# A decoder layer with a product-key expert stage: the two gate buffers of the V stage placed 128 bytes further on

## The reference, cut to what matters

```python
q = (xt @ w_pq)                                  # queries
s = einsum('thpd,hpkd->thpk', q, sub_keys)       # scores against 2 x 128 keys per head
... top-k, experts, gates = softmax(top_s)
u = take(expert_u, experts); act = gelu(einsum('tkd,td->tk', u, x))
v = take(expert_v, experts); y = einsum('tk,tkd->td', gates * act, v)
return rmsnorm(x + y, final_norm_gain)
```

## Time and profile before

| | |
|---|---|
| median of three runs | 2114.12 us (2106.12 to 2117.99) |
| the profiled execution | 2107.04 us |
| its span in the profile | 2105.3 us |
| PE busy | 2017.8 us, 96% |
| POOL, DVE, ACT busy | 1092.2, 1175.0, 903.8 us |
| granted clock of PE, mean | 0.982 of full speed |
| read from memory | 378.15 MB, 182 GB/s over the span |

### The profile page before, as it was taken

How to read it: one execution, slowest core, us unless ns; L and a number is a source line. 1 busy time by engine, 2 the same in 40 slices (tenths; PEclk the granted TensorE clock), 3 DMA queues, 4 the chain that set the end, 5 groups by cost and what they waited for, 6 DMA issues and landing times.

```text
span 2105.3 us, 36148 instructions
## 1 busy us (share of the span) xinstructions
PE 2017.8 (96%) x12814; PEld 1813.3 (86%) x12814; DVE 1175.0 (56%) x1942; ACT 903.8 (43%) x1132; POOL 1092.2 (52%) x450
## 2 busy tenths in 40 slices
PE   7798798997999999999999999999999999999996
PEld 6686687886899999999999999988888888888885
DVE  6568638125362993168888885035555555555555
ACT  6233234454543444544444444444444444444443
POOL 7576566785697888888888888850000000000001
PEclk9899899998999999999999999999999999999998
DMA  8343456554565666665555556676666665666563
GB/s 317 126 150 119 128 167 196 152 183 139 162 206 171 192 195 192 190 190 180 177 175 177 179 178 181 194 256 190 193 193 189 189 190 191 193 190 192 189 190 119
DMA packets 104753, 383.31 MB, mean 182 GB/s; under 512 B 12144, under 2 KB 12656, under 8 KB 103408
## 3 DMA queue, kind: packets, MB, share of 16 engines
q1 hardware_dynamic: 101232, 365.50, 55.1%
q10 hardware_dynamic: 3456, 16.89, 2.2%
HBM read 378.15 MB, written 4.19 MB: 182 GB/s over the span
## 4 chain that ended last, share of the span: by engine, by line
PE 69%; POOL 18%; issue 12%; DVE 1%; POOLq 0%; ACT 0%; DVEq 0%; ACTq 0%
PE ps L1215 22%; PE ps L1214 22%; PE ps L1213 22%; POOL wlo L363 18%; PE ps L1495 1%; PE ps L1469 0%; POOLq L362 0%; DVE x_back L1168 0%; DVE stats L634 0%; ACT big L608 0%; DVE stats L1179 0%; DVE big L1173 0%; POOLq L366 0%; ACT x_back L615 0%; PE ps L1521 0%
## 5 line engine op out<-in xcount | busy, mean ns | idle before, releaser
L363 POOL TENSOR_TENSOR wlo<-raw,whi 128x1024 fp32r<-128x1024 f32 x444 | 1086.3, 2450 | 314.7 <-ACT whi L413 311.1
L413 ACT ACTIVATE whi<-raw 128x1024 fp32r<-128x1024 f32 x436 | 462.4, 1062 | 768.4 <-PE ps L1215 765.6
L1213 PE MATMUL ps<-xh,whi 128*128 128x256 f32 x2176 | 601.6, 276 | 0.8 <-POOL wlo L363 0.8
L1214 PE MATMUL ps<-xl,whi 128*128 128x256 f32 x2176 | 600.8, 276 | 0.0
L1215 PE MATMUL ps<-xh,wlo 128*128 128x256 f32 x2176 | 600.8, 276 | 0.0
L1140 DVE TENSOR_TENSOR wlo<-raw,whi 128x1024 fp32r<-128x1024 f32 x248 | 304.3, 1227 | 336.6 <-ACT whi L566 336.6
L566 ACT ACTIVATE whi<-raw 128x1024 fp32r<-128x1024 f32 x256 | 271.1, 1059 | 390.5 <-PE ps L1215 390.5
L1213 PEld LDWEIGHTS ps<-xh,whi 128*128 128x128 f32 x2176 | 408.5, 188 | 1.2 <-issue 1.1
L1214 PEld LDWEIGHTS ps<-xl,whi 128*128 128x128 f32 x2176 | 408.5, 188 | 0.1
L1215 PEld LDWEIGHTS ps<-xh,wlo 128*128 128x128 f32 x2176 | 408.4, 188 | 0.0
L1215 PE MATMUL ps<-whi,gate_lo 128*128 128x512 f32 x1024 | 403.5, 394 | 0.0
(11 more groups left out here) (195 smaller groups left out, 1838.6 us busy)
## 6 DMA issues: line engine op xcount, KB each, us to landing
raw<-in_w_u SPq DMA_DIRECT2D x256, 512.0 KB, 3.5
raw<-in_w_v SPq DMA_DIRECT2D x256, 512.0 KB, 3.5
raw<-in_w_front SPq DMA_DIRECT2D x180, 512.0 KB, 3.5
big<-in_x_t ACTq DMA_DIRECT2D x4, 512.0 KB, 9.4
big<-in_x ACTq DMA_DIRECT2D x4, 512.0 KB, 5.6
big<-in_mem ACTq DMA_DIRECT2D x4, 512.0 KB, 5.5
big<-in_mem_t ACTq DMA_DIRECT2D x2, 1024.0 KB, 6.2
big<-in_x ACTq DMA_DIRECT2D x2, 1024.0 KB, 7.1
```

Source lines behind the costliest of these rows:

```text
L363: nc.gpsimd.tensor_tensor(wlo[:, j % SPL, :], raw[:, j % RAW, :], whi[:, j % SPL, :], ALU.subtract).then_inc(lo_done, 1)
L413: nc.scalar.activation(whi[:, j % SPL, :], raw[:, j % RAW, :], ACT.Copy).then_inc(hi_done, 1)
L1213: nc.tensor.matmul(out_ap, sh, mh, start=start, stop=False)
L1214: nc.tensor.matmul(out_ap, sh, ml, start=False, stop=False)
```

## The change

A buffer of 32 float32 (128 bytes), which nothing reads or writes, is put ahead of `gate_hi`, and the filler behind `gate_lo` is made 32 float32 shorter. So `gate_hi` and `gate_lo` move by 128 bytes, from offset 192 to offset 64, and all other buffers keep their places: `xh` and what follows start where they did, and the one-hot rows, which are laid out by an allocation of their own, too. No instruction is added, removed or moved, and no wait changes; every line number below the edit is one higher.

```diff
         of_u.close()
+        sb("gate_skew", [P, 32])
         gate_hi = sb("gate_hi", [P, 2, T], F32R)
         gate_lo = sb("gate_lo", [P, 2, T], F32R)
-        sb("rest_of_gates", [P, 576])
+        sb("rest_of_gates", [P, 544])
```

## The result

| | before | after |
|---|---|---|
| median of eight runs | 2114.7 us (2106.1 to 2118.0) | 2127.7 us (2118.0 to 2129.5) |
| ratio | | 1.0064, 95% interval 1.0044 to 1.0084 |
| profiled execution, span | 2107.04, 2105.3 us | 2118.00, 2116.2 us |
| first and last matmul of V | 1383.97, 2086.89 us | 1381.33, 2097.89 us |
| spacing in V | 228.9 ns | 233.3 ns |

The account below looks back on a forecast made before the run. PE's own pace was taken to bound the kernel, busy 96% of the span. V's spacing falling to 220.0 ns saves 27.3 us, other parts nothing: ratio 0.9870 times 2114.1 gives 2087 us, range 2078 to 2122.

Parts of the forecast that it names:

- That V is bound by PE's own pace: V stage: PE waits for nobody, so a change in its 228.9 ns matmul spacing passes to the end in full.
- the writes of the gate buffers: ACT and DVE writing the moved gates: even half as long again, covered by PE's work, cost nothing.
- That the period is 256 and the distance counts: PE's operand reads: the extra depends on stationary offset less moving offset, modulo 256; V goes from -64 to +64.
- They differ by 4.45 ns: Front and U, 256 columns: extras 11.1 at -64 and 6.7 ns at +64, laid to the sign of the distance.
- rows 6: Trace rows of the front's 256-column matmuls, `xh` stationary, distance -64: spacing 117.8 ns, extra 11.1.
- The four fit one simple form: All matmuls: fixed 6.7 ns, plus 4.45 per 256 columns at -64; V would fall to 220.0 ns, saving 27.3 us.
- rival B: V stage: half the gain, only the part beside the weight load goes, 4.45 ns a matmul, 13.7 us, 2100 us; chance 0.18.
- Rival C: V stage: slower, moving read meets weight load, at least 4.45 ns a matmul, 13.7 us, 2128 us; chance 0.17.
- rows 7: Trace rows of U's 256-column matmuls, weights stationary, `xh` moving, distance +64: spacing 113.3 ns, extra 6.7.
- Rival A: V stage: no change, period 128 or less, or the extra belongs to the moving operand alone; 2114 us, chance 0.29.
- rows 8: Trace rows of six 512-column matmuls at 1.2 GHz, 0.426 us apart without extra, taken to show an operand-fetch limit.
- a place in memory costs nothing: PE's operand reads: reading of the Trainium skill that speaks against any effect, making the sum 0.

Follow-up runs that it names:

- both half loads: V's stationary operands 64 columns instead of 128, against the changed kernel (gates at 64) and the one before (192): V spacing 232.7 and 228.3 ns.

## Why the prediction was wrong, step by step

**That V is bound by PE's own pace: right.** Every change of the spacing came through to the end in full. 13.6 us in V, 13.5 us by the ratio (0.64% of 2114). The tail, the writes of the gate buffers, U and the front cost nothing, as said.

**That the period is 256 and the distance counts: right.** The first was read from two stages that lie 256 apart, and the run 256 bytes on confirms it. The run with everything 64 bytes on shows the second.

**"They differ by 4.45 ns. What differs in kind is which of two operands is stationary, and with it the sign of the distance": this is the step that failed.** The difference between the earlier trace rows is not one between two arrangements. It is one between two paces, 113.3 and 117.8 ns, either of which a stretch of 256-column matmuls takes up and then keeps, with one placement. The tile of rows 6 has 113.3 in the profiles of the changed kernel and of the gates at 128, and U has 117.8 for its first stretch in six profiles (gates at 0 the second time, 128, 160, 256 bytes on, and both half loads) where `xh` was not moved relative to the weights. I had one execution, took two stretches that stood at different paces, and read the difference as a property of the code. The run with `xh` at 64 even agreed with the false rule in all its numbers. What the runs show in its place: at +64 V has 233.3 ns, an extra of 20.0 instead of the 6.7 that the rule gave, and U's 113.3 at the same distance says nothing on V.

**"The four fit one simple form": a chance fit.** Three extras and two constants. The form gave 220.0 ns, and nothing under 226.7 was seen with 512 columns. The argument against it was in my own rival B, that a form had to hold from 256 to 512 columns: it doesn't. Distance 0 is best at 512 and worst at 256, and 64 has the lowest value seen at 256 and is near the worst at 512.

**Rival C had the outcome, by luck.** Its mark was a spacing above 230 and its lower price 4.45 ns a matmul, 13.7 us, 2128 us; measured were 4.44 ns, 13.6 us, 2127.7. Its mechanism, though, is not shown. By it the moving read runs "into the place where the load began" because it starts close behind that place. Then distance 0, where the two begin together, should be bad as well, but it measured 226.7, the best, and 128 gained only 0.9 ns on 64. Its price was the 4.45 ns between rows 6 and rows 7, which belongs to two paces of 256-column matmuls. That V grew by the same 4.44 ns was not derived from anything, and no run shows why. What I held against it, that U has this distance and the smallest extra, is the failed step again. It had 0.17 by that argument, and the range ended at 2122, below its time.

**Rival A fell** with the first new placement. PE reads the gate buffers only in its weight loads. The writes of ACT and DVE into the gates move with them too, but they aren't the cause: between 252 and 272 us of the front nothing writes `xh` or `xl`, and the spacing there is 226.7 with `xh` at 0 and 233.3 at 64 and at 224, as in V. So the effect must come through the load beside the moving stream, and yet not in proportion to its length. What remains open is which circuit makes the steps, and why odd multiples of 32 stand at the top; the runs give the table and no law. Nor do rows 8 show that fetching operands is the limit: they show that the extra is gone at the lower clock, which a fixed cost hidden behind slower columns would do as well.

## What to carry to other kernels

The pace of a stream of matmuls at full clock can hang on the distance between the stationary and the moving operand modulo 256, here by 3.4% with 512 moved columns (226.7 to 234.3 ns) and by 5.9% with 256 (113.3 to 120.0), with no wait anywhere. If PE is the bound, try a few offsets per form of matmul and read the spacing of the starts. Do not carry a good distance from one form to another, and do not derive it from two stretches of one profile. First see in a second execution whether the stretch repeats. If it doesn't, the times of whole runs come in clumps, and the stage's own spacing tells what a single time can't.

## What the runs showed of the hardware that was not expected

- Most paces are a round number of cycles. At 2.4 GHz 226.7 ns are 544 cycles, 233.3 are 560, 228.9 are 549.3, which is 1648 for three. 113.3 are 272 and 120.0 are 288. Above the number of columns that is 32, 48, 37.3, 16 and 32 cycles. A steady pace can be a cycle over several matmuls: in V before, three intervals of 226, 229 and 232 ns follow each other without end. The 232.4 and 234.3 ns at 128 and 96 are 557.7 and 562.3 cycles, and there the intervals repeat after seven matmuls.
- A stretch of 256-column matmuls has two such paces at one placement, keeps the one it settles in until the stream is interrupted (the U stage for 1870 matmuls), and this makes 8 us of scatter in a program of one core at a granted clock of 0.982 to 0.983. Stretches of 512 columns in the front have two as well (228.9 and 233.3 ns at 192).
- One load in three at distance 64 gave all matmuls the mean spacing of 64 (one execution).
- "SBUF — State Buffer" of the Trainium skill, section "SBUF: two separate sides", says that TensorE never waits on anyone at its ports. Between engines nothing here contradicts that: with ACT and DVE at work beside it, V has the same pace to 0.01 ns in four executions at distance 192. But the measurement decides against what I took from it, that a place in memory costs nothing: the move by 128 bytes cost 4.44 ns a matmul.
